# Two transformer blocks on one core: the opening's modulation in six blocks, x turned by products with a diagonal of its roots

## What is computed

```python
cond = jax.nn.silu(c)
mod = cond @ w_mod + b_mod                     # 2048 -> 6 x 2048
shift_a, scale_a, gate_a, shift_m, scale_m, gate_m = split(mod, 6)
h = rmsnorm(x, pre_mix_g) * (1.0 + scale_a) + shift_a
proj = h @ w_in                                # q_lat, kv_lat, k_rope, hq, f, f, hi, hg
```

## Time and profile before

| | us |
|---|---|
| median of 3 runs | 2635.12 (2635.02 to 2637.05) |
| the profiled execution | 2635.88 |
| its span in the trace | 2634.10 |
| TensorE busy | 2573.9 (98%) |
| VectorE busy | 1825.0 (69%) |
| ScalarE busy | 1217.4 (46%) |

### The profile page before, as it was taken

The page is one execution under the profiler, slowest core; times in us unless marked ns, Lnnn a source line. Parts: engine busy times, 40 slices in busy tenths (PEclk is TensorE's granted clock), DMA queues, the critical chain, the costliest instruction groups (busy, mean ns, idle before and its releaser), DMA issues.

```text
span 2634.1 us, 39750 instructions
## 1 busy us (share of the span) xinstructions
PE 2573.9 (98%) x15041; PEld 2161.6 (82%) x15041; DVE 1825.0 (69%) x2292; ACT 1217.4 (46%) x1568; POOL 56.0 (2%) x83
## 2 busy tenths in 40 slices
PE   6999999999999999999999999999999999999998
PEld 3678877778888888888888888888888888888887
DVE  6788899888854466645659898796656656555444
ACT  4354634564434444444544444475644444444443
POOL 2100000020000000000010000000000000000000
PEclk9999999999999999999999999999999999999999
DMA  9988885858866666666566655566466666666665
GB/s 388 359 286 301 280 299 183 308 195 290 282 213 198 193 189 186 191 194 190 169 206 184 199 164 169 169 200 203 151 195 189 186 188 186 189 191 208 192 194 157
DMA packets 156476, 567.09 MB, mean 215 GB/s; under 512 B 17997, under 2 KB 18418, under 8 KB 155456
## 3 DMA queue, kind: packets, MB, share of 16 engines
q1 hardware_dynamic: 151200, 548.47, 64.9%
q0 software_dynamic: 4832, 16.68, 1.8%
q10 hardware_dynamic: 320, 0.25, 0.0%
HBM read 563.22 MB, written 2.11 MB: 215 GB/s over the span
## 4 chain that ended last, share of the span: by engine, by line
PE 48%; DVE 3%; ACT 0%; issue 0%; DVEq 0%; ACTq 0%
PE ps L869 22%; PE ps L866 11%; PE ps L886 5%; PE ps L887 5%; PE ps L888 5%; DVE w_lo L1852 1%; DVE pr L1941 0%; PE ps L967 0%; PE ps L993 0%; DVE x_tok L2123 0%; DVE tmp L1961 0%; DVE pr L1969 0%; ACT w_hi L1368 0%; PE ps L923 0%; PE ps L985 0%
## 5 line engine op out<-in xcount | busy, mean ns | idle before, releaser
L1852 DVE TENSOR_TENSOR w_lo<-w_raw,w_hi 128x1024 fp32r<-128x1024 f32 (+1 forms) x870 | 1052.0, 1215 | 662.0 <-ACT w_hi L1365 344.6
L869 PE MATMUL ps<-acts,w_hi 128*128 128x512 f32 x4096 | 1320.8, 398 | 11.7 <-DVE acts L2143 5.7
L866 PEld LDWEIGHTS ps<-acts,w_lo 128*128 128x128 f32 x4096 | 770.6, 188 | 169.3 <-issue 1.0
L1368 ACT CAST w_hi<-w_raw 128x1024 fp32r<-128x1024 f32 (+1 forms) x542 | 563.7, 1044 | 643.4 <-PE ps L869 569.5
L866 PE MATMUL ps<-acts,w_lo 128*128 128x256 f32 x4096 | 829.0, 279 | 0.3 <-issue 0.3
L869 PEld LDWEIGHTS ps<-acts,w_hi 128*128 128x128 f32 x4096 | 640.5, 189 | 33.0 <-issue 12.7
L1365 ACT CAST w_hi<-w_raw 128x1024 fp32r<-128x1024 f32 x328 | 339.3, 1040 | 470.2 <-PE ps L888 407.7
L886 PE MATMUL ps<-w_hi,ff 128*128 128x512 f32 x864 | 336.3, 389 | 0.0
L888 PE MATMUL ps<-w_hi,ff 128*128 128x512 f32 x864 | 336.1, 389 | 0.0
L887 PE MATMUL ps<-w_lo,ff 128*128 128x512 f32 x864 | 336.1, 389 | 0.0
L886 PEld LDWEIGHTS ps<-w_hi,ff 128*128 128x128 f32 x864 | 162.2, 188 | 34.6 <-issue 0.8
(11 more groups left out here) (333 smaller groups left out, 1524.9 us busy)
## 6 DMA issues: line engine op xcount, KB each, us to landing
w_raw<-in_down SPq DMA_DIRECT2D x216, 512.0 KB, 4.2
w_raw<-in_gate_up SPq DMA_DIRECT2D x176, 512.0 KB, 4.1
mod_w<-in_w_mod SPq DMA_DIRECT2D x128, 512.0 KB, 5.6
w_raw<-in_up SPq DMA_DIRECT2D x128, 512.0 KB, 4.3
w_raw<-in_in_cg SPq DMA_DIRECT2D x96, 512.0 KB, 4.0
w_raw<-in_out SPq DMA_DIRECT2D x64, 512.0 KB, 4.4
w_raw<-in_in_qfb SPq DMA_DIRECT2D x48, 512.0 KB, 5.4
mod_w<-in_w_mod_first SPq DMA_DIRECT2D x32, 512.0 KB, 9.5
```

The source lines that it names most:

```text
L866: mm = pe.matmul(ps[:, bank, 0:T], w_lo[:, slot, k, c:c + P], lin_.act[:, kk, 0, :], start=False, stop=at_last and n == 0, skip_group_chec ...
L869: mm = pe.matmul(ps[:, bank, :], w_hi[:, slot, k, c:c + P], lin_.act[:, kk, :, :], start=at_first, stop=at_last and n == 1, skip_group_che ...
L1368: act.copy(w_hi[:, slot, 0:kn, 0:lin_.width], w_raw[:, slot, 0:kn, 0:lin_.width]).then_inc(hi_ready, 1)
L1852: dve.tensor_tensor(low[cut], raw[cut], high[cut].bitcast(F32), ALU.subtract).then_inc(lo_ready, 1)
```

## The change

`PAIRS` becomes 1, 1, 2, 2, 1, 1: the first block of two pairs is cut into two of one pair each. Pieces 0 to 7 now have four rows of 256 columns. The later blocks keep their shapes and are counted one up. The lists are written anew: which chunks TensorE runs inside a block (`INSIDE`, by block), how many are kept over to the next but one, and where the remainders stand. `FIRST_CHUNK` is 12 operations, three narrow pieces.

x is no longer scaled by ScalarE. VectorE multiplies the identity by the roots (`x_diag`, two operations behind piece 1's shift), and `turn_x` multiplies x itself by this diagonal, 16 true float32 products a half. Half 0 is turned behind piece 2, half 1 behind the columns of block 0. VectorE applies block 0 behind piece 5 of the new order (`APPLIED_BEHIND`), with its first chunk's remainder ahead. The two long parts of `rope_angles` move to new block 2, behind its pieces 2 and 6; the masks' copy stands behind its piece 4.

```diff
-PAIRS = 2, 2, 2, 1, 1
+PAIRS = 1, 1, 2, 2, 1, 1
-INSIDE = {(8, 6): (1, 2, 4, 6), (4, 6): (1, 2, 3, 3), (4, 3): (1,)}
-LATER_LO = {(8, 6): (0, 1, 3, 5), (8, 3): (0,), (4, 6): (0, 1, 3, 3), (4, 3): (0,)}
-FIRST_LO = {8: (6, 7), 4: (3, 3)}
-FIRST_CHUNK = 8
+EARLY_TURNS = 2
+APPLIED_BEHIND = 2
+INSIDE = {1: (2, 3), 2: (2, 5), 3: (1, 2, 4, 6), 4: (1, 2, 3, 3), 5: (1,)}
+LATER_LO = {1: (3, 3), 2: (0,), 3: (0, 1, 3, 5), 4: (0, 1, 3, 3), 5: (0,), 6: (0,)}
+FIRST_LO = {1: (3, 3), 2: (6, 7), 3: (6, 7), 4: (3, 3), 5: (3, 3)}
+ROPE_AT = (0, 0), (2, 2), (2, 6)
+FIRST_CHUNK = 12
...
             def turn_x(half):
+                pe.wait_ge(*t_1.scaled(2))
...
-                    pe.wait_ge(*t_1.scaled(4 * half + quarter + 1))
...
-                        mm = pe.transpose(ps[:, quarter, i * P:(i + 1) * P],
-                                          t_1.xh[:, half, k * P:(k + 1) * P], ident)
+                        mm = pe.matmul(ps[:, quarter, i * P:(i + 1) * P], t_1.xh[:, half, k * P:(k + 1) * P],
+                                       x_diag[:, half, :], start=True, stop=True)
...
                     scale_piece(0, p)
-                    if p == 2:
+                    if p == 1:
                         pe.wait_ge(late_loads, 16 * N_LATE)
                         turn_vectors(range(1, V_TILES))
-                    if p in (5, 6):
-                        turn_x(p - 5)
+                    if p == EARLY_TURNS:
+                        turn_x(0)
                 keep_warm(7, 4)
                 block_columns(0)
+                turn_x(1)
                 for block in range(1, BLOCKS):
                     n = PIECES[block]
                     for p in range(n):
-                        if p < KEPT and block >= 2:
-                            opening_chunk(block - 2, BLOCK_CHUNKS[block - 2] - KEPT + p)
+                        kept = BLOCK_CHUNKS[block - 2] - len(INSIDE[block - 1]) if block >= 2 else 0
+                        if p < kept:
+                            opening_chunk(block - 2, BLOCK_CHUNKS[block - 2] - kept + p)
...
-                act.wait_ge(*t.stat(3))
-                for i, half, cut in sorted(pieces(), key=lambda p: p[1]):
-                    act.activation(t.xh[:, half, cut], x_tok[:, half, cut], ACT.Identity,
-                                   scale=x_root[:, half:half + 1]).then_inc(t.scaled.sem, 1)
...
+                park_x(0)
+                scale_row(0)
+                round_chunk(phases[0], 0, 0, True)
+                park_x(1)
                 act.wait_ge(x_parked, 8)
...
                     if block:
                         take_block(block - 1)
+                    if block == 1:
+                        remainder(phases[0], 0, 0)
+                    elif block:
                         apply_block(block - 1)
                     for p in range(n):
+                        if (block, p) == (1, APPLIED_BEHIND):
+                            apply_block(0)
                         if block < BLOCKS:
                             shift_piece(block, p)
-                        if block == 0 and p == 1:
+                        if (block, p) == (0, 1):
                             inverse_root(x_sums, x_root[:, :], t_1.stat, t_1.squared)
+                            for half in range(2):
+                                dve.tensor_scalar(x_diag[:, half, :], ident, x_root[:, half:half + 1], None,
+                                                  ALU.mult).then_inc(t_1.scaled.sem, 1)
...
-                        if block == 0 and p in (0, 3, 4):
-                            rope_angles((0, 3, 4).index(p))
-                        if block == 1 and p == 4:
+                        if (block, p) in ROPE_AT:
+                            rope_angles(ROPE_AT.index((block, p)))
+                        if (block, p) == (2, 4):
...
-                    dve.wait_ge(x_parked, 8)
+                    dve.wait_ge(x_parked, 5)
```

More of the change, by code:

```diff
@@ L645, in __init__ @@
                 self.stat = count("x_stat", 3 * halves)
-                self.scaled = count("xh_scaled", 8)
+                self.scaled = count("xh_scaled", 2 if halves == 1 else 8)
                 self.turned = count("xh_turned", DT)
@@ L1675, in start @@
                 move_vectors(range(1, V_TILES))
-                for half in range(2):
-                    for quarter in range(4):
-                        act.wait_ge(*t_1.turned(8 * half + 2 * quarter + 2))
-                        act.copy(x_turned[:, 4 * quarter:4 * quarter + 4, half * P:(half + 1) * P],
-                                 ps[:, quarter, :].rearrange("p (i t) -> p i t", i=4)).then_inc(x_parked, 1)
+                park_x(0)
+                scale_row(0)
+                round_chunk(phases[0], 0, 0, True)
+                park_x(1)
                 act.wait_ge(x_parked, 8)
                 for block in range(BLOCKS):
-                    for c in range(KEPT):
-                        round_chunk(phases[0], 0, 3 * FIRST_PAIR[block] + c, True)
-                    scale_row(block)
+                    if block:
+                        for c in range(KEPT):
+                            round_chunk(phases[0], 0, 3 * FIRST_PAIR[block] + c, True)
+                        scale_row(block)
                     act.wait_ge(gains_ready, block + 1)
@@ L1689, in start, with park_x @@
                                        bias=mods[:, k:k + 1]).then_inc(t_1.hi.sem, 1)
-                    for c in range(KEPT, BLOCK_CHUNKS[block]):
+                    for c in range(KEPT if block else 1, BLOCK_CHUNKS[block]):
                         round_chunk(phases[0], 0, 3 * FIRST_PAIR[block] + c, True)
-                    if block == 0:
+                    if block == ROPE_AT[-1][0]:
                         act.wait_ge(angles, 2)
                         act.activation(cos_sin[:, :, :], ang[:, 0:2, :], ACT.Sin).then_inc(sines, 1)
+            def park_x(half):
+                for quarter in range(4):
+                    act.wait_ge(*t_1.turned(8 * half + 2 * quarter + 2))
+                    act.copy(x_turned[:, 4 * quarter:4 * quarter + 4, half * P:(half + 1) * P],
+                             ps[:, quarter, :].rearrange("p (i t) -> p i t", i=4)).then_inc(x_parked, 1)
             def scale_row(block):
@@ L2341, in start @@
                         if 0 < block < BLOCKS:
[L2342 removed]
+                            for c, at_piece in enumerate(FIRST_LO[block]):
                                 if at_piece == p:
                                     remainder(phases[0], 0, 3 * FIRST_PAIR[block] + c)
[L2345 to L2347 removed]
+                        if (block, p) in ROPE_AT:
+                            rope_angles(ROPE_AT.index((block, p)))
+                        if (block, p) == (2, 4):
                             dve.wait_ge(late_loads, 16 * N_LATE)
                             link(dve.tensor_copy(masks[:].rearrange("p a l t -> p (a l t)"), masks_i[:, :]))
[L2350 to L2352 removed]
             def shift_piece(block, p):
```

15 lines of the change are left out of this document (6 added, 9 removed).

## The result

| | before | changed |
|---|---|---|
| median, us | 2638.81 (7 runs, 2635.02 to 2643.12) | 2645.37 (7 runs, 2640.99 to 2647.74) |
| profiled execution, us | 2635.88 | 2645.37 |
| its span, us | 2634.10 | 2643.6 |
| TensorE busy, us | 2573.9 | 2574.5 |
| piece 15's columns start | 65.35 | 71.25 |

The change makes the kernel slower: the ratio of the times is 1.0025, with an interval of 1.0014 to 1.0035. That is +6.6 us where +1.2 was forecast. The median of the kernel before is itself 3.7 us above that of its first three runs, so the difference counts, not the bare 2645.37.

The account below looks back on a forecast made before the run. The full DMA queues set the start of new block 3's columns, with 46 us of TensorE's own work behind. That start moves from 92.7 to 93.9, +1.2 us, giving 2636.3 us; 8-in-10 range 2632.2 to 2641.0.

Parts of the forecast that it names:

- The front: Opening up to piece 15: VectorE idle about 26 to 31 us, turn halves 5.5 and 4 us, VectorE's block ending at 70.2.
- The first emptying: DMA queues ahead of piece 8, asked for late at 35.8 us: 2 to 2.5 us of empty queues.
- second emptying: DMA queues near 77 us, piece 20 waiting for piece 16: about 1.5 us more; 2 us in the slower rival.
- rival B: Block 0's columns to piece 23: VectorE's chain holds to the end, +6 to +9 us, 2641 to 2644; 10%.
- What the empty queues cost: Opening's queues: 2 to 2.5 and about 1.5 us empty, two chunks asked for early; piece 22 lands about 89.5, not 88.56.
- the point: Start of new block 3's columns, behind piece 23's sum, 92.74 us before: forecast about 93.9, +1.2 us.
- VectorE by itself has caught up: VectorE up to piece 23: its own work gives 92.3 us, since it stood idle for 10.5 of 39.6 us before.
- Behind it nothing changes: From new block 3's columns to the next phase: TensorE's own 46 us stay, later phases only shift.
- The sum: Whole kernel: 93.9 - 92.7 = +1.2 us, nothing changed behind; median 2635.12 + 1.2 = 2636.3.
- columns of block 0 later than about 36 us: Sign in the opening, 31 us forecast: the slower rival, VectorE's chain holding to the end, decides from there.
- Rival A: Opening: new block 3's columns come earlier through a better front and fewer early chunks, -1 to -4 us, 2633; 19%.
- C: Opening up to piece 23: it lies wholly with the queues, old and new at their pace, +-0.5 us, 2635.1; 22%.

Follow-up runs that it names:

- e3: Changed kernel with ten warming products ahead of block 2's columns and four ahead of block 3's; 2641.83 us, ratio 1.0022 to the kernel before.
- e5: Kernel before with only the two long rope parts moved, to behind pieces 10 and 14; 2642.14 us, ratio 1.0023 to the kernel before.
- e1: Changed kernel with both long rope parts moved back to block 0, behind pieces 2 and 3; 2641.19 us, ratio 1.0018 to the kernel before.
- e9: Changed kernel with the long rope parts behind pieces 3 and 10, none behind piece 14; 2638.85 us, ratio 1.0007 to the kernel before.
- e12: The changed kernel measured again, unchanged, beside two other runs; 2642.23 us, ratio 1.0020 to the kernel before.
- e4: Changed kernel with the piece's product ahead of the kept-over chunk on TensorE; 2643.81 us, ratio 1.0020 to the kernel before.
- e6: Changed kernel with pieces 4 and 5 early on TensorE and VectorE, first long rope part behind piece 7; 2643.37 us, ratio 1.0018 to the kernel before.
- e7: Kernel before with two and three warming products ahead of the columns of old blocks 1 and 2; 2640.53 us, ratio 1.0006 to the kernel before.
- e11: Changed kernel, pieces 4 and 5 early, rope behind pieces 7 and 10, piece before kept chunk, two warming products at blocks 2 and 3; 2638.37 us, ratio 1.0006.
- e2: Kernel before with only the turning of x done by true products with the diagonal, ScalarE's scalings gone; 2638.26 us, ratio 1.0005 to the kernel before.
- e8: Changed kernel with rope parts in block 0, four warming products at blocks 2 and 3, piece ahead of kept chunk; 2638.50 us, ratio 0.9999.

## Why the prediction was wrong

**The front** was right. VectorE stood idle for 5.26 us until 31.27 (5.3 until 31.1 were laid out); the turn's halves took 6.00 and 3.82 us (5.5 and 4.0); chunk 0 began at 38.67 (39.1); piece 15's sum started at 69.65 and its columns at 71.25 (70.2), the wait that I named.

**The first emptying** near 36 us was put at 2 to 2.5 us and was some 0.8 in its window (343 GB/s in 35 to 40), 1.3 over the whole stretch.

**The step that failed is the second emptying**, "about 1.5 more near 77". It measured 4.6 us. The working had the columns done at 72.1, the kept chunk and piece 16 behind that at full clock, and so piece 16 used near 76. Piece 16 was used at 80: columns 1.05 us later than 70.2, then 1.6 us more for the columns themselves (3.4 us for both groups instead of 1.8) and 1.4 for the kept chunk (4.3 us from its start to that of the next piece instead of 2.9), mostly at 1.2 GHz. I had the price of the half clock, the row that shows it behind a wait, and put it into rival B alone, though my own layout held a wait of the same kind, only longer. The forecast itself had the idle time that brings it. e3 takes just this away, and the hole shrinks.

**What the empty queues cost** was sized wrongly too. The forecast had 3.5 to 4 us of them and made +1.2 us at the point out of that, with chunks asked for early to cover the rest. The runs give nearly all of it to the point: 6.2 us of empty queues made 5.1 (changed), 5.6 made 4.8 (e5, 406 and 350 GB/s), 3.6 made 2.5 (e1), 1.9 made 1.0 (e9, 389 and 403 GB/s). By these rows the forecast's own 3.5 to 4 us would have been some 2.5 to 3 at the point.

**"VectorE by itself has caught up"** was right and beside the point: it waited again for landings at 88.4. The pieces it waited for were the late ones. What counts isn't when an engine catches up, but how late it frees the slot in between: SyncE asks for piece 20 when piece 16 is used, 80.10 instead of 71.74, and no later idle time brings the queues' lost time back. The point was forecast at 93.9 and came at 97.80.

**"Behind it nothing changes"** failed by 1.7 us: 47.49 us from the point to the next phase, not 45.80. The half clock behind the point lasted 6.8 us instead of 3.4; 3.4 us more at half speed are 1.7 us of work. e3, without it, has 44.3.

**The sum**: +5.1 at the point and +1.7 behind it give +6.75 at the next phase. The profiled span is 9.5 us longer. Of the other 2.75, 0.8 lies in two waits of TensorE for VectorE's remainders, 1.35 us at 157.69 (0.98 before) and 0.45 at 216.42 (none before). The other 0.5 that has come up by 482 us, where VectorE is 8.1 us late, is open. At 530 us it is 10.3 us late (its first `xh<-y,row`, at 530.0 and, before, 519.7). In between a chunk of in_out landed late, which ScalarE waited for and then, through VectorE's remainder, TensorE (first line before, the others changed):

```profile
479.27 1.05 ACT L1365 CAST w_hi<-w_raw 128x1024 fp32r<-128x1024 f32 x1 [2.90 <-DMA w_raw<-in_out]
```
```profile
489.56 1.04 ACT L1370 CAST w_hi<-w_raw 128x1024 fp32r<-128x1024 f32 x1 [5.11 <-DMA w_raw<-in_out]
501.49 0.50 PE L889 MATMUL ps<-w_hi,att_out 128*128 128x512 f32 x1 [2.31 <-DVE w_lo L1860]
```

The same place is 7.1 us late in e12, without such a wait, so these 2.2 us don't come with every execution of the change. A stretch of half clock at 569 us, which before doesn't have, costs nothing: VectorE's last operation on `x_tok` there starts at 571.9, 10.3 us late as well, and `gate_col` at 769.6 is 10.1 late. Such a stretch comes at 561 to 580 us in seven of the thirteen profiles here and in the others not (before, e3, e4, e6, e7, e11).

**Rival B** comes nearest: "VectorE's chain holds to the end", with a second emptying and half clock behind the idle time, +6 to +9 us. It had 10%. That its size is right is partly luck. The second emptying (2 us there, 4.6 measured) and the half clock came, but the turns at 1.2 GHz did not (6.00 and 3.82 us, close to the forecast's 5.5 and 4), and VectorE's chain did not hold to the end, since it waited for landings again from 88.4. Two readings in it were wrong: the 9.5 us to landing that B takes as the longest is the median of 32 transfers, and its terms of 5.4, 2 and 1.7 us add up to 9.1, not to 5 to 8. (A's middle, from which the range starts, is 2632.6, not 2632.2.) Its condition was misread, too: "columns of block 0 later than about 36 us" wasn't needed; they came at 30 to 31. It decides at piece 15, and there by whether the rope stands between two pieces. Rival A's extra room didn't exist; C's price is what e11 shows at the point, and e9 but for 1 us, once nothing stands behind piece 14.

**The cause**, as far as shown: of the change's parts the late rope alone is enough for the loss (e5, both long parts in the old kernel, +6.5 us at the next phase), and of its two places it is the one behind piece 14 (e9, emptied in the new kernel, 7.2 us earlier). In the time the two agree: 1.0023 for e5, as for the changed kernel, and 1.0007 for e9 beside 1.0020 for e12. The diagonal costs nothing (e2), narrow blocks and new lists with no rope behind piece 14 cost 1.0 us at the point through the first emptying (e9), which earlier pieces 4 and 5 take away (e11), and nothing that the time can tell. The half clock carries some 3 to 5 us of the opening's 6.75: e3 gives back 4.8, of which 1.5 is from a stretch that the kernel before has too. e3 is one profile with other small differences (its first stretch has 396 GB/s, not 391), so these are bounds of an estimate. Left open: why e3's median doesn't follow its opening, and why waits alike in length are followed by half clock of different length.

## What to carry over

Before filler work is moved into another's idle time, look not at how much idle time a stretch has, but at what is next in line at that very place: filler ahead of an instruction that will wait for a landing cost next to nothing here (e9), the same filler ahead of one whose data is down and for which another engine waits was paid in full (e5). Where transfers reuse slots, follow the lateness one turn further, to the request that the late use holds back, and price the empty queue; a later idle time of the engine doesn't give it back. And where the sum itself makes TensorE wait for several us, the half clock behind that wait belongs into the sum, not into a rival.

## What was not expected of the hardware

A column group of products with one column each (L1099, 8 instructions) took 1.05 us at full clock and 1.86 at half. Around a wait of 4.8 to 5.5 us the clock was 0.50 for 6.8 to 13.6 us, in five kernels (changed, e12, e5, e4, e6), and the wait of 1.37 us at the point of before was followed by 3.4 us of it. The length of the wait doesn't tell that of the stretch: 1.71 us (changed, the point) and 1.76 (e1, piece 15) were followed by 6.8, 1.82 (e9, piece 15) by 3.4, and 1.11 (e9, the point) by none. With warming products in the wait it stayed at 1.00 at these places (e3, e7, e8), but not with two of them at piece 15 in e11.

A true f32 product of 128x128 by 128x128 takes 0.24 us (3.82 for 16), a turn in transpose mode 0.12: 1.9 times, as the prediction took from the earlier trace rows. The "four times" for f32 that the Trainium skill has ("TensorE: Matmul & The Clock Gate", section Terms) isn't seen at this size; the measurement decides.

Opening and time go together only roughly. In eight of the twelve rows of the table the opening's gain or loss lies within the interval of the time; in e3, e6, e7 and e11 it lies outside, by 1.5 us in e3 and by up to 0.9 in the others. e2's opening is that of before to 0.05 us and its median 1.9 us higher, e11's is 1.7 us shorter and its median 1.4 higher. Differences of 1 to 2 us in the opening can't be told from the time.
